# Stack copies of a hybrid attention block moved from the SyncE queue to the GpSimd queue

## What is computed

```
h    = rmsnorm(x) * pre_norm
proj = h @ w_in                      # q, k, v of three groups, memory q, forget logits, gate (2048 wide)
o_a  = differential attention        # 4 heads, two softmaxes each: p0 - lam*p1, T5 bias, then an RMS norm
o_b  = stick-breaking attention      # 8 heads of 64: sigmoids and a reverse running sum along the keys
o_c  = forgetting attention          # 8 heads of 64: softmax(q.k + c_q - c_k), c = cumsum(log sigmoid)
o_m  = attention to 256 memory rows  # 4 heads of 128
y    = concat(o_a, o_b, o_c, o_m) * silu(gate)
out  = x + rmsnorm(y @ w_out) * post_norm
```

## Time and profile before

| What | us |
|---|---|
| median of 3 runs | 2605.59 (2602.4 to 2607.44) |
| the profiled execution, its own time | 2597.89 |
| its span, first to last instruction | 2596.1 |
| PE busy | 2344.3 (90%) |
| DVE, ACT, POOL busy | 1676.6, 1598.9, 1348.5 (65%, 62%, 52%) |
| DMA engines, mean busy share of both queues | 65.2% and 2.6% |

### The profile page before, as it was taken

The page is one execution under the profiler, slowest core; times in us unless marked ns, Lnnn a source line. Parts: engine busy times, 40 slices in busy tenths (PEclk is TensorE's granted clock), DMA queues, the critical chain, the costliest instruction groups (busy, mean ns, idle before and its releaser), DMA issues. The chain is left out here.

```text
span 2596.1 us, 71707 instructions
## 1 busy us (share of the span) xinstructions
PE 2344.3 (90%) x26710; PEld 1597.2 (62%) x26710; DVE 1676.6 (65%) x4701; ACT 1598.9 (62%) x4309; POOL 1348.5 (52%) x2128
## 2 busy tenths in 40 slices
PE   5699999998999999969999999699999995899998
PEld 4476676656766666558666665486666663644443
DVE  7646699876556997765559987656489885311111
ACT  5457888665568885655688866557788765312211
POOL 6435555776565566765655667756656565100000
PEclk9799999998999999989999999899999997899999
DMA  6359989645599887455998874567988833854341
GB/s 198 96 120 158 164 159 157 137 91 111 130 179 174 161 143 160 88 99 126 179 171 157 143 164 92 101 129 153 180 160 151 160 75 61 209 147 114 81 114 49
DMA packets 987798, 353.00 MB, mean 136 GB/s; under 512 B 833956, under 2 KB 972204, under 8 KB 987436
## 3 DMA queue, kind: packets, MB, share of 16 engines
q1 hardware_dynamic: 980856, 330.58, 65.2%
q0 software_dynamic: 6592, 17.83, 2.6%
HBM read 72.38 MB, written 35.23 MB: 41 GB/s over the span
## 5 line engine op out<-in xcount | busy, mean ns | idle before, releaser
L1574 POOL TENSOR_TENSOR rows<-rows 128x512 f16<-128x512 f32 (+3 forms) x864 | 867.5, 1020 | 646.7 <-ACT rows L1496 640.2
L1339 PE MATMUL job<-wt,big 128*128 128x128 f16 x10752 | 686.5, 220 | 0.8 <-DVE planes L1589 0.4
L1339 PE MATMUL job<-big,wt 128*128 128x512 f16 x2688 | 663.2, 380 | 8.2 <-PEq L760 5.1
L1339 PEld LDWEIGHTS job<-wt,big 128*128 128x128 f16 x10752 | 630.8, 98 | 46.0 <-DVE gate_s L1686 0.7
L1496 ACT CAST rows<-rows 128x512 f16<-128x512 f32 (+3 forms) x864 | 459.1, 545 | 215.0 <-DMA rows<-rows 171.4
L1393 PEld LDWEIGHTS mixed<-values,rows 128*128 128x128 f16 x8544 | 384.9, 100 | 216.5 <-DMA rows<-rows 107.1
L1393 PE MATMUL mixed<-values,rows 128*128 128x64 f16 (+1 forms) x8544 | 440.6, 202 | 83.4 <-DMA rows<-rows 63.7
L1378 PE MATMUL scores<-stack 128*128 128x512 f16 (+3 forms) x1600 | 435.5, 352 | 63.3 <-DVE mx L1645 42.8
L1518 ACT ACTIVATE rows<-rows,neg_max 128x512 f32<-128x512 f32 (+3 forms) x704 | 445.5, 634 | 76.2 <-DVE neg_max L1655 76.0
L1641 DVE TENSOR_SCALAR_CACHE_REDUCE rows<-scores 128x512 f32<-128x512 f32 (+3 forms) x640 | 360.3, 582 | 121.6 <-POOL rows L1574 92.6
L1339 PEld LDWEIGHTS job<-big,wt 128*128 128x128 f16 x2688 | 246.8, 98 | 257.7 <-issue 9.0
(11 more groups left out here) (155 smaller groups left out, 2630.7 us busy)
## 6 DMA issues: line engine op xcount, KB each, us to landing
stack<-planes SPq DMA_DIRECT2D x160, 192.0 KB
ws<-w_in SPq DMA_DIRECT2D x56, 512.0 KB, 4.7
y_halves<-y_out_halves SPq DMA_DIRECT2D x64, 256.0 KB, 2.7
rows<-rows SPq DMA_TRANSPOSE x864, 3.3
rows<-x SPq DMA_DIRECT2D x16, 512.0 KB, 5.2
temps<-w_out POOLq DMA_DIRECT2D x64, 128.0 KB, 3.6
out_weight_halves<-temps POOLq DMA_DIRECT2D x64, 128.0 KB, 3.8
big<-out_weight_halves SPq DMA_DIRECT2D x16, 512.0 KB, 10.9
```

The costliest lines, as they stand in the source:

```text
L1339: last = nc.tensor.matmul(dst, lhs, rhs, start=(k0 == 0 and q == 0), stop=(k1 == KT and q == len(pairs) - 1))
L1574: nc.gpsimd.tensor_tensor(halves_of(tau, 1, w), scored(plan.chunk_at(g, m, k0), 0, w), halves_of(tau, 0, w), ALU.subtract).then_inc(low_po ...
```

## The change

The function `stacks` is moved out of the SP program and takes the engine that issues its DMAs; POOL's list calls it. The rank of `stacks` moves from SP's table (-0.49115, ahead of everything) to POOL's (3.0, behind `lo`, `wo` and `ylo_pool`, ahead of `root`). Other numbers of the planner change with it: `convert` and `square` on ACT and `norm` on DVE (which ranks `variance` too) fall back, `near_in` on SP moves up, `AHEAD["forget"]`, `SLACK` and two margins fall.

```diff
-    "act": {"beta": -1.02044, "convert": 0.09860, "square": 1.56409, "y_hi": 1.90013, "stick": 4.11322,
...
+    "act": {"beta": -1.02044, "y_hi": 1.90013, "convert": 2.39679, "stick": 4.11322, "job": 4.42172,
+            "hi": 4.85840, "exp": 6.05197, "square": 8.72906},
...
-            "post": 3.72902, "scan": 4.02979, "norm": 6.33521, "widen": 6.61046, "copy": 7.20142},
-    "pool": {"lo": 0.09877, "wo": 2.26711, "ylo_pool": 2.95644, "root": 4.79189},
-    "sp": {"stacks": -0.49115, "store": 1.06927, "pairs": 1.90869, "sums": 2.46883, "turn": 2.93844,
-            "strip": 7.81310, "near_in": 13.10196},
+            "post": 3.72902, "scan": 4.02979, "widen": 6.61046, "norm": 7.11509, "copy": 7.20142},
+    "pool": {"lo": 0.09877, "wo": 2.26711, "ylo_pool": 2.95644, "stacks": 3.00000, "root": 4.79189},
+    "sp": {"store": 1.06927, "pairs": 1.90869, "near_in": 2.43885, "sums": 2.46883, "turn": 2.93844,
+            "strip": 7.81310},
...
-AHEAD = {"mem": 1.00000, "stick": 0.75620, "diff": 0.14564, "forget": 0.68448}
-SLACK, LATE = 17.35582, 11.80560
+AHEAD = {"mem": 1.00000, "stick": 0.75620, "diff": 0.14564, "forget": 0.53223}
+SLACK, LATE = 16.34821, 11.80560
...
+        def stacks(eng, t, c, load):
...
+            if load == 0:
+                if t:
+                    eng.wait_ge(s_full, plan.last_chunk[plan.stack_user(t)])
+                eng.wait_ge(j_free, last_group_job(t, c) + 1)
...
-                    if op == "stacks":
-                        stacks(*args)
...
+                    if op == "stacks":
+                        stacks(pool, *args)
```

More of the change, by code:

```diff
@@ L59 @@
     "pe": {"mix": 3.42686, "score": 5.99980, "gate": 6.18532, "project": 7.37012},
-    "act": {"beta": -1.02044, "convert": 0.09860, "square": 1.56409, "y_hi": 1.90013, "stick": 4.11322,
-            "job": 4.42739, "hi": 4.85840, "exp": 6.05197},
+    "act": {"beta": -1.02044, "y_hi": 1.90013, "convert": 2.39679, "stick": 4.11322, "job": 4.42172,
+            "hi": 4.85840, "exp": 6.05197, "square": 8.72906},
     "dve": {"lo_dve": 1.52081, "weigh": 1.69925, "ylo": 1.93750, "combine": 2.12124, "low": 2.34038,
-            "post": 3.72902, "scan": 4.02979, "norm": 6.33521, "widen": 6.61046, "copy": 7.20142},
-    "pool": {"lo": 0.09877, "wo": 2.26711, "ylo_pool": 2.95644, "root": 4.79189},
-    "sp": {"stacks": -0.49115, "store": 1.06927, "pairs": 1.90869, "sums": 2.46883, "turn": 2.93844,
-            "strip": 7.81310, "near_in": 13.10196},
-}
-AHEAD = {"mem": 1.00000, "stick": 0.75620, "diff": 0.14564, "forget": 0.68448}
-SLACK, LATE = 17.35582, 11.80560
+            "post": 3.72902, "scan": 4.02979, "widen": 6.61046, "norm": 7.11509, "copy": 7.20142},
+    "pool": {"lo": 0.09877, "wo": 2.26711, "ylo_pool": 2.95644, "stacks": 3.00000, "root": 4.79189},
+    "sp": {"store": 1.06927, "pairs": 1.90869, "near_in": 2.43885, "sums": 2.46883, "turn": 2.93844,
+            "strip": 7.81310},
+}
+AHEAD = {"mem": 1.00000, "stick": 0.75620, "diff": 0.14564, "forget": 0.53223}
+SLACK, LATE = 16.34821, 11.80560
 MARGIN = {
-    "mix": 0.37422, "score": 0.17580, "gate": 0.00000, "project": 0.09693, "hi": 0.00000,
-    "lo": 0.00000, "copy": 0.00000, "exp": 1.07124, "weigh": 0.00000, "norm": 1.22740,
+    "mix": 0.37422, "score": 0.17580, "gate": 0.00000, "project": 0.00000, "hi": 0.00000,
+    "lo": 0.00000, "copy": 0.00000, "exp": 1.07124, "weigh": 0.00000, "norm": 1.08636,
     "y_hi": 0.53563}
@@ L1215, in load_row @@
                                    y_dram[i * P:(i + 1) * P].rearrange("s k h f -> s (k h f)")).then_inc(landed, 16)
+        def stacks(eng, t, c, load):
+            at = slice(c * BANK, (c + 1) * BANK)
+            if load == 0:
+                if t:
+                    eng.wait_ge(s_full, plan.last_chunk[plan.stack_user(t)])
+                eng.wait_ge(j_free, last_group_job(t, c) + 1)
+            forget = UNIT[t].kind == "forget"
+            h, part = divmod(load, 3 if forget else 2)
+            if h == 2:
+                eng.dma_start(stack[64:67, 1:6:3, at], c_scale).then_inc(stacked[c], 16)
+                return
+            src = planes[h * 64:h * 64 + 64, :, at]
+            dst = stack[:, 3 * h:3 * h + 3, at]
+            if part == 0:
+                eng.dma_start(dst[0:64], src[:, 0:3, :]).then_inc(stacked[c], 16)
+            elif part == 2:
+                eng.dma_start(hk_c[0:64, h, at], src[:, HK, :]).then_inc(stacked[c], 16)
+            elif forget:
+                eng.dma_start(dst[64:128, 0:3:2], src[:, 3:0:-2, :]).then_inc(stacked[c], 16)
+            else:
+                eng.dma_start(dst[64:128], src[:, 3:0:-1, :]).then_inc(stacked[c], 16)
         with nc.Block() as block:
@@ L1226, in load_weights @@
                                  w_cols[:, :, at:at + P]).then_inc(w_in_sem[n % 2], 16)
[L1228 to L1249, removed]
                 def out_weights():
```

## The result

The changed kernel takes 2689.1 us (median of 4 runs, 2677.24 to 2696.2), the kernel before 2606.52 on the same chip: a ratio of 1.0323, 95% interval 1.0299 to 1.0347. It is slower by 83 us, outside the range that I gave and past the rival that went furthest. The profiled execution took 2677.24 us.

What follows compares the result with a forecast made beforehand. The prediction took PE, busy 90% of the span, as the bound, so only its idle time could change. Its terms -5 + 2 - 8 + 3 = -8 us, off the median of 2605.59, gave 2598 us, range 2579 to 2624.

Steps and rivals of the forecast that it cites:

- the rival that went furthest: "Descriptors starve", the rival with the slowest forecast time, 2626 us; chance 0.05.
- What POOL gets: POOL takes over 240 copies, 163 us of issue; later landings are mostly covered: +2 us, ends -2.1 and 28.
- SP sheds -5 us: With some 150 us of copy issues off SP, turns behind copy groups come sooner: -5 us, ends 0 and 11.
- The shared engines: All queues' DMAs run on the same 16 engines, so moving the copies saves at most SP's issue time.
- POOL's issues: Each stack copy takes POOL 0.68 us to issue, 163 us for 240; POOL busy near 1510 us.
- The cover of 8 to 12 us: Added project matmuls on PE before later stick and diff scores, 8 to 12.6 us, cover landings 3.5 us later.
- The diff ends, -8 us: At diff units' ends, root and converts fall behind, so `lo`s and copies start earlier: -8 us, ends 0 and 18.
- The fill, +3 us: Project work done earlier leaves PE less to fill later waits in diff units: +3 us, ends 0 and 14.5.
- POOL is late: Rival: `lo`s and copies hold each other up at eight stick and diff starts, +28 us, 2624 us; chance 0.26.
- Descriptors starve: Rival: DVE holds up POOL's DMA issues, 56 us of POOL, half reaching PE, 2626 us; chance 0.05.
- My test for "wrong": PE waiting tens of us for the stack or longer for `lo`, POOL copies over 1 us, or diff-end idle grown.

Runs made afterwards that it cites:

- numbers: The change's new planner numbers with the stack copies back on SP: 2589.32 us, 0.9942 of the kernel before; repeated at 2587.64 us, 0.9923.
- pads: As numbers, copies on SP, with POOL doing the change's waits and a tiny DMA per copy: 2593.51 us, 0.9958 of the kernel before.
- ghost: thin with POOL's tiny DMAs made as large as the stack copies, into spare DRAM, nobody waiting: 2633.98 us, 1.0126 of the kernel before.
- thin: pads with SP's copies cut to 4 bytes a row from the second lane on, leaving work out: 2575.14 us, 0.9899 of the kernel before.
- first: The change with the copies ranked ahead of the `lo`s on POOL (-0.49115 for 3.0): 2654.73 us, 1.02 of the kernel before.
- the two defer runs: numbers with c2 and c3 copies of stick and diff units planned 4 or 8 us later on SP: 2581.75 and 2582.22 us.
- echo: numbers, but scores wait for a tiny DMA that POOL issues after a group's landing: 2627.2 us, 1.0096 of the kernel before.

## Why the prediction was wrong

The step that failed is in "What POOL gets": I priced the copies on POOL by their issue time and by three `lo`s at a unit start, +2 us with 28 at most, and gave their new queue no price. The term measured 100 us (the change against `numbers`). POOL's issues and waits as such are some 4 of them (`pads`). The other 96 are the traffic on another queue beside the turns, which costs 41 us more than on SP's queue in three lanes (`ghost`, `thin`, `pads`), and the copies' place in POOL's list, of which a better order alone takes back 34 us (`first`).

- **SP sheds -5 us.** Not shown. The stretches behind the groups were more idle than others, but no run shows that taking the copies off SP gave it back. What the copies cost on SP is the 18 us between `thin` and `pads`, which are the bytes and their landing, and perhaps the 6 us of the two defer runs, which is the order.
- **The shared engines.** I named them as a bound on the gain and did not ask what the turns lose. The Trainium skill, "DMA: Bandwidth & Descriptors", has the rule that I should have weighed, in "Queues, rings and completion order": each DMA engine takes turns between the rings that have work, packet by packet. By that rule, moving 38 MB out of the turns' ring (their queue's line on each engine) takes away the planned order and makes both share each engine while copies are in flight. The trace agrees in what turns lose, 5.71 against 3.85 us; the taking of turns itself is not to be seen in it.
- **POOL's issues.** 240 copies; those of L1232 took 0.644 us at the median, where I said 0.68, and POOL is 1474 us busy, not 1510. `pads` shows that this and POOL's waits cost some 4 us.
- **The cover of 8 to 12 us.** From the end of the last scores of the unit before, the first scores of stick units came after 15.7 to 22.3 us in the change, against 8.0 to 8.5 before. The landing took 4 to 8 us from the last issue and the issues of a group were spread over 5.7 to 8.3 us, where I had added 3.5 us. Still the cover held for the copies: in u1 the scores came as c0 landed (301.8 and 301.93 us), in u5, u9 and u13 c0 had landed 5.0 to 5.8 us earlier. What it did not cover is the turns: ahead of these four starts PE waited 1.8, 2.6, 5.0 and 5.3 us for them in its mixes, where it had waited 1.1 at most.
- **The diff ends, -8 us.** The direction was right and the size too small. From u2's first scores to u3's, and for the other three diff units likewise, the kernel before takes 605.5 us, `numbers` 571.7, the change 572.1. Some of these 33 us are project work done earlier, for the whole of `numbers` gains 16 to 19. PE's waits for DVE are 65.9 us in `numbers` (39.0 and 26.9), where I said 65 for the change; there they are 77, about the 76 of before.
- **The fill, +3 us.** With the diff ends: the other units of `numbers` give back some 23 us of what its diff units gain (forget 11, stick 3, mem 9, from the profiled executions, whose spans are 12 us apart). The sum of both terms, -5 in mine, was -16 to -19.
- **Rivals.** "POOL is late" had the right sign and, in part, the right place: copies behind `lo`s, 34 us by `first`. Its limit of 3.5 us at eight starts was wrong: the groups of forget were late too (14 to 15 us of issue for three of them), PE's wait for turns grew most in forget units, and the rival had no turns in it. "Descriptors starve" did not happen:

```profile
L1232 POOL DMA_DIRECT2D stack<-planes x96: 610/644/792, 134.3 to 2128.8; - x96
```

My test for "wrong" was PE waiting for the stack for tens of us. It never did, and the kernel was slower all the same: the planner had put other work ahead of the scores, and what PE waited for was turns, in the mixes.

What stays open: how the 96 us divide exactly. Bytes on the other queue rather than on SP's (41 us in three lanes, 54 by my estimate for four, 41 times 4/3) and delay (38 us in `echo`) come to about the size, but each was measured without the other, the ghost's bytes went to DRAM, and the delay of `echo` was of my choosing. Also open is why GpSimd's queue costs more than ScalarE's.

## What to carry to other kernels

Moving DMAs to another queue can slow those that stay. Before splitting a queue, ask which transfer in it somebody waits for at each moment: here a small urgent turn landed in 3.9 us with a copy of its own queue in flight and in 5.7 us with one of another queue. And separate a change into its parts before judging it: here a good replan, worth 16 to 19 us, was hidden under a move that cost 100.

## What was not expected of the hardware

- A transpose beside copies of another queue: 5.7 us from issue to landing on average and up to 21.3, against 3.9 and 6.7 where both are in one queue, though the DMA engines were 0.77 busy on the mean from 130 to 2190 us. The longest issue of a chunk's turn was 13.1 us, 3.3 before; whether the copies or the load of weights in its own queue held it is not shown.
- A copy of 192 KB on GpSimd's queue landed 5.5 us after its issue at the median, up to 13.3, and was moved in 4 KB packets whether its rows had 512 or 1024 bytes.
- ScalarE, 62% busy, lost 90 us to 240 issues with their waits, GpSimd, 52% busy, some 4 us: the busy share did not tell the cost. That it is what stands behind the issue is my guess.
